# Strassen's seven products for 6 of 8 down-projection chunks in a TensorE-bound FP32 kernel

## What is computed

```python
def sq_relu_mlp(xn, w_in, w_out):          # xn 512x1024, w_in 1024x4096, w_out 4096x1024
    h = jax.nn.relu(xn @ w_in)
    return (h * h) @ w_out

for i in range(DEPTH_2):                   # 2 layers
    ...
    h = h + mix
    h = h + sq_relu_mlp(rms_norm_2(h, norm_mlp_g[i]), mlp_w_in[i], mlp_w_out[i])
```

## Time and profile before

| what | us |
|---|---|
| median of 3 runs | 1740.84 |
| lowest of the runs | 1740.7 |
| span of the profiled execution, first to last instruction | 1738.9 |
| busy TensorE matmul / weight load | 1729.0 / 1408.5 |
| busy VectorE / ScalarE / GpSimd | 839.2 / 765.2 / 985.6 |

### The profile page before, as it was taken

One profiled execution on the slowest core, in us unless ns is written; L12 is line 12 of the kernel. 1 busy time (PEld: TensorE's weight loads), 2 busy tenths in 40 slices (PEclk: granted clock), 3 DMA queues, 4 the chain that ended last, 5 costly groups with the idle time before them and its releaser, 6 DMA issues.

```text
span 1738.9 us, 25414 instructions
## 1 busy us (share of the span) xinstructions
PE 1729.0 (99%) x8321; PEld 1408.5 (81%) x8321; DVE 839.2 (48%) x1617; ACT 765.2 (44%) x1242; POOL 985.6 (57%) x1179
## 2 busy tenths in 40 slices
PE   9999999999999999999999999999999999999998
PEld 7778888888888778888888888877777888888887
DVE  5875755555211454665141414567777641414143
ACT  5665555555322444344232323446565532323243
POOL 5543655555555334367575757655555675757574
PEclk9999999999999999999999999999999999999999
DMA  5211322222224222222222222322321222222222
GB/s 193 70 67 62 105 101 96 96 96 97 97 88 148 95 67 83 73 85 97 97 97 97 96 97 96 139 94 83 116 103 57 90 97 97 96 97 96 97 96 97
DMA packets 48629, 167.49 MB, mean 96 GB/s; under 512 B 5376, under 2 KB 6672, under 8 KB 48528
## 3 DMA queue, kind: packets, MB, share of 16 engines
q1 hardware_dynamic: 48272, 166.05, 27.5%
q10 hardware_dynamic: 288, 0.52, 0.1%
HBM read 164.31 MB, written 2.24 MB: 96 GB/s over the span
## 4 chain that ended last, share of the span: by engine, by line
PE 97%; DVE 1%; DMA 1%; ACT 1%; POOL 0%; issue 0%; SPq 0%; DVEq 0%
PE bank L637 18%; PE bank L539 14%; PE bank L545 14%; PE bank L540 14%; PE bank L934 5%; PE bank L935 5%; PE bank L939 5%; PE bank L655 3%; PE bank L661 3%; PE bank L656 3%; PE bank L982 2%; PE bank L981 2%; PE bank L987 2%; PE bank L1204 1%; PE bank L1233 1%; PE bank L1216 1%
## 5 line engine op out<-in xcount | busy, mean ns | idle before, releaser
L435 POOL TENSOR_TENSOR w_lo<-stage,w_hi 128x256 fp32r<-128x256 f32 x1128 | 929.2, 856 | 688.5 <-ACT w_hi L1353 397.5
L1353 ACT ACTIVATE w_hi<-stage 128x1024 fp32r<-128x1024 f32 x282 | 298.0, 1057 | 467.3 <-PE bank L540 339.2
L539 PE MATMUL bank<-xn_hi,w_hi 128*128 128x512 f32 x544 | 211.7, 389 | 0.0
L540 PE MATMUL bank<-xn_lo,w_hi 128*128 128x512 f32 x544 | 211.7, 389 | 0.0
L539 PE MATMUL bank<-arena,w_hi 128*128 128x512 f32 x496 | 192.9, 389 | 0.0
L540 PE MATMUL bank<-arena,w_hi 128*128 128x512 f32 x496 | 192.9, 389 | 0.0
L637 PE MATMUL bank<-xn_hi,w_hi 128*128 128x512 f32 x464 | 189.0, 407 | 0.0
L637 PE MATMUL bank<-xn_lo,w_hi 128*128 128x512 f32 x464 | 181.8, 392 | 0.0
L934 PE MATMUL bank<-xn_hi,w_hi 128*128 128x512 f32 x352 | 137.1, 389 | 0.0
L935 PE MATMUL bank<-xn_lo,w_hi 128*128 128x512 f32 x352 | 136.9, 389 | 0.0
L545 PE MATMUL bank<-xn_hi,w_lo 128*128 128x512 f32 x544 | 135.0, 389 | 0.0
(11 more groups left out here) (342 smaller groups left out, 2848.1 us busy)
## 6 DMA issues: line engine op xcount, KB each, us to landing
stage<-weights SPq DMA_DIRECT2D x283, 512.0 KB, 3.2
bias<-table SPq DMA_DIRECT2D x11, 896.0 KB, 5.6
out<-z SPq DMA_DIRECT2D x8, 256.0 KB, 2.0
x<-x_in SPq DMA_DIRECT2D x3, 512.0 KB, 8.1
bias<-swa_table SPq DMA_DIRECT2D x4, 256.0 KB, 3.6
...
```

Source lines behind the costliest of these rows:

```text
L435: ins = nc.gpsimd.tensor_tensor(w_lo[:, p_, ks], stage[:, p_, ks], w_hi[:, p_, ks].bitcast(F32), ALU.subtract)
L539: pe.matmul(G[p_][:], w_hi[:, p_, k], hi[:, k], start=(first and k == ks[0]), stop=False)
L540: mm = pe.matmul(G[p_][:], w_hi[:, p_, k], lo[:, k], start=False, stop=False)
L1353: act.activation(w_hi[:, p_], stage[:, p_], ACT.Copy).then_inc(hi_ready, 1)
```

## The change

In each of the two MLPs the down projections of chunks 0, 1 and 2 (`N_FAST` is 3 of `N_CH` 4) are done in another way; chunk 3 and all up tiles stay. The output of such a chunk, 1024 x 512, is made in four *quads*. Quad j covers the output rows of x tiles 2j and 2j+1 and all 1024 hidden features. Its weights are four blocks of 128x512: A11, A12, A21, A22 (first or second output tile, even or odd tiles of hidden features), and the hidden tiles are cut in the same way by even or odd tile and by the first or second 256 tokens: B11, B12, B21, B22. Seven products of such blocks or of their sums give the quad, in this order of slots: A11, S1 = A21 + A22, A12, S2 = S1 - A11, S4 = A12 - S2, S3 = A11 - A21, A22. The right factors are B11, T1, B21, T2, B22, T3, T4. T1 = B12 - B11, T3 = B22 - B12, T2 = B22 - T1, T4 = B21 - T2.

Each product is 4 x 3 matmuls of 256 columns, 12 where a tile had 24 of 512, and 28 products take the place of 8 tiles. Where the work lies:

- SP loads a quad as two transfers of 512 KB, even quads into `prob`, odd quads into `stage`.
- DVE makes the four sums (`quad_sum`) and the low part of S1 and S2 (`quad_low`); ACT makes the high part of all seven slots (`quad_high`); POOL makes the low part of the other five.
- There is one slot of each kind, so slot k of the next quad is filled after product k of this one.
- The products gather in three PSUM regions: R1 (two banks in turn; A11, then S2 and S3 on top), R5 (S1, then S4 on top), R2 (A12, later A22). DVE adds a region to `x` after each product (`added`), and PE waits with S2 until A11 is added, with S4 until S1 is, with S3 until S2 is, with the next A12 until all seven are.
- After an up tile of these chunks DVE does relu and `rstd` at once out of PSUM, ACT squares, DVE makes one 256-column difference (even tiles) or three (odd tiles), ACT makes the high copies, DVE the low ones.

Up tiles are called 0 to 7 below, quads 0 to 3. The diff, cut to its core:

```diff
 # POOL
+            def mlp2_splits(l):
+                for n in range(N_FAST):
+                    t = T_MLP2[l] + KD * n
+                    q = QUADS * (N_FAST * l + n)
+                    split_los(t, t + 6)
+                    quad_lows(q, (HI_A11, HI_A12))
+                    split_lo((t + 6) // 2, 0)
+                    split_lo((t + 6) // 2, 1)
+                    pool.wait_ge(tile_done, t + KD - 1)
+                    quad_lows(q, (HI_S4,))
+                    pool.wait_ge(tile_done, t + KD)
+                    quad_lows(q, (HI_S3, HI_A22))
+                    for j in range(1, QUADS):
+                        quad_lows(q + j, (HI_A11, HI_A12, HI_S4, HI_S3, HI_A22))
 # PE
+            def product(l, n, q, k, quads):
...
+                if quads[0] == 0:
+                    pe.wait_ge(slot_high, N_HIGH * q + k + 1)
+                    read = N_PROD * q + {HI_A11: -N_PROD, HI_S1: -2, HI_A12: 0, HI_S2: 1, HI_S4: 2, HI_S3: 4, HI_A22: 3}[k]
+                    if read > 0:
+                        pe.wait_ge(product_added, read)
...
+                for i in quads:
+                    w = slot_hi[k][:, i * P:(i + 1) * P]
...
+                    pe.matmul(region, w, fc_hi[:, i, f], start=(fresh and i == 0), stop=False, skip_group_check=True)
+                    pe.matmul(region, w, fc_lo[:, i, f], start=False, stop=False, skip_group_check=True)
...
+                for i in quads:
+                    w = slot_lo[k][:, i * P:(i + 1) * P]
+                    mm = pe.matmul(region, w, fc_hi[:, i, f], start=False, stop=(i == QUADS - 1), skip_group_check=True)
+            def fast_down(l, n):
+                every, most, last = list(range(QUADS)), list(range(QUADS - 1)), [QUADS - 1]
...
+                    if j == 0:
+                        product(l, n, q, HI_A12, most)
+                        product(l, n, q, HI_S2, most)
+                        product(l, n, q, HI_A12, last)
+                        product(l, n, q, HI_S2, last)
 # ACT, in the loop over the up tiles e
+                        if e < KD - 2:
+                            split_hi(t // 2 + i + 1, p_)
...
+                        act.wait_ge(evac[p_], t // 2 + i + 1 - MLP2_SKIP[l])
+                        act.activation(tmp[:, p_], tmp[:, p_], ACT.Square).then_inc(squared, 1)
...
+                        if e == 4:
+                            quad_high(q, HI_A11)
+                            quad_high(q, HI_S1)
+                        elif e == 5:
+                            quad_high(q, HI_A12)
+                        elif e == 6:
+                            act.wait_ge(hi_free, t + KD - 1)
+                            act.wait_ge(lo_ready, t + KD - 1)
+                            quad_high(q, HI_S2)
+                            quad_high(q, HI_S4)
 # DVE, after the up tiles
+                for j in range(QUADS):
...
+                    more = j < QUADS - 1
+                    added(x0[:, 0:HS], r1, HI_A11)
+                    if more:
+                        quad_sum(v + 1, 0)
+                    added(x1[:, HS:S], r5, HI_S1)
+                    if more:
+                        quad_sum(v + 1, 1)
+                        quad_sum(v + 1, 2)
+                    added(x0[:, 0:HS], r2, HI_A12, 1)
+                    if more:
+                        quad_sum(v + 1, 3)
+                        quad_low(v + 1, HI_S1)
+                    added(x0[:, HS:S], r1, HI_S2)
+                    if more:
+                        quad_low(v + 1, HI_S2)
+                    added(x0[:, HS:S], r5, HI_S4, 4)
```

More of the change, by code:

```diff
@@ L105, with program @@
 LAMBDA_INIT = 0.8 - 0.6 * math.exp(-0.3 * 1)
[L108 removed]
+def program(nc, x_in, params, consts, buckets, swa_table, weights, pairs, tables, out):
     with ExitStack() as ctx:
@@ L505, in _ @@
                 split_t(t)
-            with pool.Fori(T_MLP2[1] // 2, N_TILES // 2) as m:
-                for p_ in range(2):
-                    split_lo(m, p_)
+            mlp2_splits(1)
+            split_los(T_MLP2[1] + KD * N_FAST, N_TILES)
             for h in range(2):
@@ L1326, in mlp2 @@
             def mlp2(l):
-                for n in range(NF2 // KD):
-                    t = T_MLP2[l] + 2 * KD * n
+                for n in range(N_CH):
+                    t = T_MLP2[l] + KD * n
                     if n == 0:
@@ L1332, in mlp2 @@
                         tiles(t, t + KD, xn_hi, xn_lo)
-                    whole = 2 * KD if t + 2 * KD < N_TILES else 2 * KD - 2
-                    with pe.Fori((t + KD) // 2, (t + whole) // 2) as m:
-                        for p_ in range(2):
-                            tile(m, p_, ff_hi, ff_lo, late=(ff_ready, NF1 + NF2 * l + KD * (n + 1)))
+                    if n < N_FAST:
+                        fast_down(l, n)
+                t += KD
+                whole = KD if t + KD < N_TILES else KD - 2
+                with pe.Fori(t // 2, (t + whole) // 2) as m:
+                    for p_ in range(2):
+                        tile(m, p_, ff_hi, ff_lo, late=(ff_ready, NF1 + N_FC * (l + 1)))
             layer_a()
@@ new lines, in mlp2 @@
+                t = T_MLP2[l] + KD * N_FAST
+                f0 = fc_at(l, N_FAST, 0)
+                with act.Fori(0, KD // 2) as i:
+                    for p_ in range(2):
+                        split_hi(i + t // 2 + 1, p_)
+                        act.wait_ge(tile_done, 2 * i + t + p_ + 1)
+                        act.wait_ge(ff_ready, 2 * i + f0 + NF1 + p_ - 1)
+                        act.activation(tmp[:, p_], G[p_][:], ACT.Relu).then_inc(evac[p_], 1)
+                        act.wait_ge(u_ready, 2 * i + f0 + p_ + 1)
+                        act.activation(ff_hi[:, bass.ds(2 * i + p_, 1)].rearrange("p o s -> p (o s)"), tmp[:, 2 + p_],
+                                       ACT.Square).then_inc(ffh_ready, 1)
@@ L2654, in mlp2 @@
                 dve.wait_ge(rstd_ready, 4 + 2 * l)
-                for n in range(NF2 // KD):
-                    t = T_MLP2[l] + 2 * KD * n
-                    f0 = NF2 * l + KD * n
+                for n in range(N_FAST):
+                    fast(l, n)
+                for n in range(N_FAST, N_CH):
+                    t = T_MLP2[l] + KD * n
+                    f0, s0 = fc_at(l, n, 0), NF2 * l + KD * n
                     def low2(i, p_):
```

291 lines of the change are left out of this document (245 added, 46 removed).

## The result

The changed kernel takes 1818.68 us (median of 4 runs, 1815.37 to 1819.14), the kernel before 1740.77: ratio 1.0445, 95% interval 1.043 to 1.0461. One of the four runs of the kernel before took 3644.3 us and tells nothing of it; the other three lie between 1740.3 and 1740.8. The forecast was 1806, range 1762 to 1846, slower.

A forecast was written before the change was run, and what follows sets the result against it. PE was taken as the bound, its matmuls filling 99% of the span. Columns -19, tile 6 +37, quad 0 +31, quads 1 and 2 +16 sum to +65: 1806 us, +3.7%, range 1762 to 1846.

The forecast's parts named there:

- Columns, -19: Down parts of six fast chunks: 336 matmuls of 256 columns replace 192 of 512, 3.2 us less per chunk, -19 us.
- Rival 5: Fast chunks: 256-column matmuls fed too slowly or weight loads not hidden, 192 ns each, +126 us; chance 0.02.
- Tile 6, 6.2 us: Up tile 6: PE waits 6.2 us for POOL's low part, queued behind A12's; six chunks, +37 us (33 to 52).
- Quad 0, 2.3 and 3.0: Quad 0: PE waits for DVE's adds of A11 (2.3) and S2 (3.0); six chunks, +31 us (22 to 43).
- sums near 0.9 each: Sign to look for in the quads: DVE's weight sums take near 0.9 us each.
- Quads 1 and 2, 1.3: Quads 1 and 2: PE waits 1.3 us before S3 for DVE's add of S2; twelve quads, +16 us (5 to 28).
- None in quad 3: Quad 3: no sums stand behind it, so PE never waits there for DVE's add.
- rival 1: Up tile 6: clock falls to 1.2 GHz in the waits, 3.4 us each, 20 in all, 1826 (or 1847); chance 0.15.
- the prediction's own last line: Wrong if tile 6 waits under 3 us, waits for `x` total under 20 us, or granted clock is not 1.00.
- Rival 2: Tile 6 and quads 0 to 2: DVE and POOL operations exclude each other in full, longer waits, 1843; chance 0.09.
- Rivals 3 and 4: 3: only tile 6 waits, 1759, chance 0.13; 4: A12's low part early, DVE keeps up, 1722, chance 0.03.
- The point of no loss: Fast chunks: the change breaks even at 3.2 us of wait per chunk in all.

The follow-up runs named there:

- e2: The changed kernel with DVE's add of S2 moved ahead of the next quad's fourth sum and low part of S1: 1789.7 us.
- e3: As e2, and quad 0's add of A11 goes ahead of DVE's 768-column low part of up tile 7: 1788.7 us.
- e5: The changed kernel with 26 extra 512-column matmuls, results unused, filling PE's wait in up tile 6 of each fast chunk: 1805.2 us.
- e6: The changed kernel with POOL's low parts of the quads made in two pieces of 256 columns instead of one of 512: 1814.3 us.
- e1: The changed kernel with POOL's low part of A12 moved behind the low parts of up tiles 6 and 7: 1784.3 us.
- e7: As e8, with POOL's low parts of quad 0's S3 and A22 held back until DVE has finished tile 7: 1748.4 us.
- e8: The changed kernel with tile 6's low part ahead of A11 and A12 on POOL, A12's high part and quad 0's adds earlier: 1745.0 us.
- e12: e9 with DVE's adds, S1's low part and the sums reordered in quads 0, 1 and 2, and A22 ahead of S3 in quad 0: 1773.8 us.
- e9: e8 with S4's products and S1's add earlier in quad 0, and the third sum behind A12's and S2's adds in quads 1, 2: 1739.8 us.

## Why the prediction was right, and where its sizes were off

**Columns, -19: right.** The 256-column matmuls stand 0.12 apart (835.50, 835.61, 835.73 in the timeline of PE), weight loads hidden. Rival 5 is out. This spacing holds in all thirteen traces of the new form, and with it the 3.2 us a chunk.

**Tile 6, 6.2 us: right.** Measured 6.14 from start to start, six times alike. POOL's low part of A12 starts at 820.71, 4.6 after tile 6's first matmul (forecast 4.8), takes 1.51, and the lows of tiles 6 and 7 take 6.41 together, 3.2 for one (3.5).

```profile
820.71 1.51 POOL L542 TENSOR_TENSOR arena<-prob,v_split 128x512 fp32r<-128x512 f32 x1 [5.27 <-ACT v_split L2046]
822.18 6.41 POOL L500 TENSOR_TENSOR w_lo<-stage,w_hi 128x256 fp32r<-128x256 f32 x8
```

**Quad 0, 2.3 and 3.0: 2.2 and 2.3.** The mechanism stands, shown by e2 and e3; the second term was 0.7 too large. I had five operations at 0.9 each. In the rows above they take 1.43, 0.68, 0.69, 1.44 and 0.68, 4.9 in all where the forecast had 4.5, but the row runs without the gaps I gave it, nearly each operation starting before the listed end of the one ahead. The "sums near 0.9 each" were right only as a mean of this row: they take from 0.68 up to 1.79, the longest beside POOL. Two slips of sums change nothing: six times 5.3 is 32 and not 31, and all slow terms at tile 6 come to 8.8 and not 8.6.

**Quads 1 and 2, 1.3: 1.01**, by the same step. None in quad 3, as said. The three kinds of wait come to 75 us, forecast 84.

**The clock: wrong.** "PE never rested more than 1.5 us there" was the row, and I kept the clock at 1.00, with half clock as rival 1 at 0.15. The granted clock was 0.983, and by the prediction's own last line ("or if the granted clock is not 1.00") it was wrong in this. The half clock came beside the forecast's waits, not in their place: 20.3 us. That rival 1 gave 20 too is luck: it had all of it at tile 6, 3.4 a chunk, where it was 2.2 on the mean (13.3 in all, and e5 bears that out), and it had nothing in quad 0, where the other 7 lie, behind waits of 2.1 and 2.2 us. The rule of the Trainium skill (TensorE: Matmul & The Clock Gate, HAM oscillation) that waits between bursts of matmuls can bring the clock to half was right here, and should have stood in the sum. So 1806 was as near as it was by errors of opposite sign, which is luck: 9 us too much of waiting, 20 too little of clock and 2 of second matmuls.

**Rival 2, DVE and POOL shut each other out in full: in part.** The lengths do reach 1.70 on the mean of one group, the sum of a DVE operation alone and a wait of a microsecond, and e6 shows them follow the length of POOL's piece. The rule of the Trainium skill (SBUF — State Buffer, SBUF: two separate sides), by which a DVE operation with two SBUF inputs and one of POOL shut each other out, fits one more row: the adds, with one of their inputs in PSUM, stay at 0.41 and 0.69 even there. But in the row between the adds DVE met POOL twice at a price of 0.75 each, not 1.3, as if an operation met only what was left of a piece; no run tests that by itself. Each kernel that packed POOL's work more tightly (e1, e7) lengthened DVE's and gave a part back.

**Rivals 3 and 4: out.** DVE did not keep up, and A12's low part was not early. The point of no loss, 3.2 us a chunk, was right, and is what e8 to e12 ran into.

**What the best order is worth.** e9 undoes all the loss and ends where it began: 0.9996, interval 0.9987 to 1.0005. Nothing tried here beats the kernel before by a measurable amount. Whether an order exists that keeps POOL's row, the adds and the sums all in time is open; even a perfect one could win no more than the 19 us of columns, 1.1%.
